# Attention probabilities as the stationary operand of the values' matmuls, softmax shares and output norms applied by token, the compressed step moved to fifth place, and the first scores issued among the latent keys' scalings

## The reference

```python
# A: 8 heads of width 64, three branches, causal:  p = softmax(q k^T * scale);  o = p v
out_a = g0 * o_cmp + g1 * o_slc + g2 * o_win    # 31 compressed keys; 512 keys; 512 keys
# B: 8 latent (mla) heads, keys and queries of width 96, values of width 64, causal
mixed = concat([rmsnorm(o_a) * out_gain_a, rmsnorm(o_b) * out_gain_b]) @ w_out
h = x + mixed                                   # then h + peer_ffn(rmsnorm(h))
```

## Time and profile before

| | |
|---|---|
| median of 3 runs | 2412.17 us (2411.32 to 2415.41) |
| the profiled execution's own time | 2410.7 us |
| its span, from first to last instruction | 2408.7 us |
| busy: PE, DVE, ACT, POOL | 98%, 71%, 35%, 46% of the span |
| attention, first scores to the B half's first products | 968.27 to 1143.83 us |

### The profile page before, as it was taken

How to read it: one execution, slowest core, us unless ns; L and a number is a source line. 1 busy time by engine, 2 the same in 40 slices (tenths; PEclk the granted TensorE clock), 3 DMA queues, 4 the chain that set the end, 5 groups by cost and what they waited for, 6 DMA issues and landing times.

```text
span 2408.7 us, 35086 instructions
## 1 busy us (share of the span) xinstructions
PE 2372.0 (98%) x12248; PEld 2033.5 (84%) x12248; DVE 1720.4 (71%) x2873; ACT 837.2 (35%) x1445; POOL 1115.0 (46%) x747
## 2 busy tenths in 40 slices
PE   8999999999999999899999999999999999999999
PEld 6888888878888887676889999999999888888887
DVE  8888785463433656876627699798886788888887
ACT  4132222100113315776224333344443333333333
POOL 7777776665666550103563788731112322222220
PEclk9999999999999999899999999999999999999999
DMA  4333323333332223100224899999999999999995
GB/s 158 97 105 105 104 95 126 134 111 108 132 117 95 88 74 121 36 1 10 70 88 127 286 311 303 301 354 347 339 342 402 383 356 349 353 358 354 346 359 200
DMA packets 181333, 490.41 MB, mean 204 GB/s; under 512 B 14848, under 2 KB 80512, under 8 KB 181248
## 3 DMA queue, kind: packets, MB, share of 16 engines
q1 hardware_dynamic: 144384, 355.12, 43.3%
q0 software_dynamic: 36864, 134.23, 14.9%
HBM read 436.86 MB, written 52.43 MB: 203 GB/s over the span
## 4 chain that ended last, share of the span: by engine, by line
PE 90%; issue 3%; POOL 3%; DVE 2%; ACT 1%; DMA 0%; SPq 0%; DVEq 0%; POOLq 0%; ACTq 0%
PE ps L690 40%; PE ps L1299 22%; PE ps L1259 17%; POOL spl L2661 2%; PE ps L1135 2%; PE ps L1280 2%; PE ps L1109 1%; POOL rare L2671 1%; PE ps L1094 1%; PE ps L874 1%; PE ps L1048 1%; PE ps L994 1%; PE ps L894 0%; PE ps L1098 0%; PE ps L1097 0%
## 5 line engine op out<-in xcount | busy, mean ns | idle before, releaser
L690 PE MATMUL ps<-hh,spl 128*128 128x512 f32 x1728 | 536.3, 390 | 4.3 <-DVE hl L2315 2.8
L1259 PE MATMUL ps<-hh,spl 128*128 128x384 f32 x2048 | 535.6, 337 | 2.9 <-POOL spl L2661 2.9
L1299 PE MATMUL ps<-spl,wsp 128*128 128x512 f32 x2304 | 523.8, 389 | 0.0
L1651 ACT ACTIVATE spl<-ring 128x1024 fp32r<-128x1024 f32 x256 | 271.9, 1062 | 678.0 <-PE ps L1299 325.6
L1299 PEld LDWEIGHTS ps<-spl,wsp 128*128 128x128 f32 x2304 | 432.0, 188 | 89.4
L2534 POOL TENSOR_TENSOR spl<-ring,spl 128x1024 fp32r<-128x1024 f32 (+1 forms) x164 | 425.6, 2595 | 13.1
L690 PEld LDWEIGHTS ps<-hh,spl 128*128 128x128 f32 x1728 | 324.3, 188 | 74.0 <-DVE hl L2315 4.2
L1259 PEld LDWEIGHTS ps<-hh,spl 128*128 128x128 f32 x2048 | 371.2, 188 | 6.3 <-issue 5.4
L2532 POOL CAST spl<-ring 128x1024 fp32r<-128x1024 f32 (+1 forms) x164 | 190.0, 1159 | 353.2 <-PE ps L690 334.6
L1259 PE MATMUL ps<-hl,spl 128*128 128x384 f32 x1024 | 342.5, 334 | 0.0
L2433 DVE TENSOR_TENSOR spl<-ring,spl 128x1024 fp32r<-128x1024 f32 x192 | 235.2, 1225 | 148.2 <-ACT spl L1651 134.3
(11 more groups left out here) (451 smaller groups left out, 3401.5 us busy)
## 6 DMA issues: line engine op xcount, KB each, us to landing
ring<-stream_in SPq DMA_DIRECT2D x134, 512.0 KB
ring<-u_in SPq DMA_DIRECT2D x128, 512.0 KB
ring<-v_in SPq DMA_DIRECT2D x128, 512.0 KB
ring<-stream_in SPq DMA_DIRECT2D x60, 704.0 KB
gelu<-gst SPq DMA_DIRECT2D x128, 192.0 KB
dense<-stage SPq DMA_DIRECT2D x12, 2048.0 KB
gl<-gelu SPq DMA_DIRECT2D x32, 768.0 KB, 7.1
gw<-dense SPq DMA_DIRECT2D x32, 768.0 KB, 9.9
```

Source lines behind the costliest of these rows:

```text
L690: m = pe.matmul(ps[:, bank, :], w[:, part, k0 + k * n:k0 + k * n + P], rhs(k), start=first and k == 0 and part == 0 and rhs is high, stop= ...
L1259: m = pe.matmul(ps[:, bank, 0:TD], w[:, part, k0 + k * P:k0 + (k + 1) * P], rhs(k), start=first and k == 0 and part == 0 and rhs is high, ...
L1299: m = pe.matmul(ps[:, bank, :], wsp[:, j % 2, part, tok], spl[:, j % 2, row, cols], start=False, stop=last and n == 2)
L1651: eng.activation(spl[:, j % 2, 0, 0:D], ring[:, j % RING, 0:D], ACT.Copy).then_inc(hi_done, 1)
```

## The change

1. **Values turned.** `values(u)` takes 128x128 tiles of turned probabilities as the stationary operand and 64 columns of V as the moving one. A slc, win or mla step on tile qt has qt+1 such matmuls, issued in pass u+3 for that step alone; cmp has one with 256 columns in place of four with 128. The result has tokens on the partitions.
2. **Shares by token.** `inverses` and `shares` are gone. `turn` waits for the exp and no longer for the shares. `weigh_head` on DVE, once for each head and branch and eight steps after its last one, takes the inverse of four sums, times the gate, and multiplies 128x256 out of PSUM; for slc and win it also adds to `oall`.
3. **Turned probabilities leave PSUM on two engines.** Tiles 0 and 1 and cmp are copied by DVE (five steps later on its list), tiles 2 and 3 by ACT (two steps later, before: four).
4. **Norms by token.** Squares with row sums run on ACT (`o_squares_of`), the inverse root makes four diagonal matrices on DVE (`turned_by`), and PE turns and scales `oall` by matmuls with them (`turned_chunk`, four of 128 columns for each of eight chunks). ACT and DVE make high and low parts straight from PSUM. POOL's squares and parts, `o_column`, `o_rows` and `o_scaled` are gone.
5. **Order.** cmp is each A head's fifth step (before: third). The scores of steps 0 to 2 stand among the last four scalings of latent keys, with their maxima on DVE (`early_bias`); only the first cmp scores wait for `mid_ready`. After the last step the first half of unit 3 stands behind the B half's `turned_chunk`.

```diff
-        HEAD_STEPS = [(SLC, 0), (SLC, 1), (CMP, 0), (SLC, 2), (SLC, 3), (WIN, 0), (WIN, 1), (WIN, 2), (WIN, 3)]
...
+        HEAD_STEPS = [(SLC, 0), (SLC, 1), (SLC, 2), (SLC, 3), (CMP, 0), (WIN, 0), (WIN, 1), (WIN, 2), (WIN, 3)]
...
+        BANK_OF = {n: 6 + (GROUPS[n][1] == "win" if n < 3 * A_H else n % 2) for n in range(GN)}
...
+        def on_dve(u):
+            return GROUPS[STEPS[u][0]][1] == "cmp" or STEPS[u][1] < 2
...
+        TURN_LAG, VALUE_LAG, WEIGH_LAG, EARLY = 2, 3, 8, 3
+        A_SQUARES, A_ROOT = A_H * PER + 6, A_H * PER + 10
+        A_TURNS = [A_H * PER + 13 + 4 * k for k in range(TT)]
...
-            def turn(n, qt):
-                u = STEP_OF[n, qt]
-                pe.wait_ge(at_scale, u + 1)
+            def turn(u):
+                n, qt = STEPS[u]
                 if u >= 2:
...
-                        v = vm[:, kt, at // 2 * P:(at // 2 + 1) * P]
-                    else:
-                        c = (kind == "win") * P
-                        v = vtok[:, kt, c:c + P]
-                    m = pe.matmul(bank[:, kt * P:], v, pt[:, wide_of(n), kt, kt * P:],
-                                  start=kind != "win" and kt == 0, stop=kind != "slc" and kt == TT - 1)
...
+                    m = pe.matmul(out_, turned[:, 0:P], vcz[:, :, g * A_D:(g + 1) * A_D], start=True, stop=True)
...
+                    for kt in range(qt + 1):
+                        if kind == "mla":
+                            v = vm[:, kt, at * B_V:(at + 1) * B_V]
+                        else:
+                            c = (kind == "win") * P + g * A_D
+                            v = vtok[:, kt, c:c + A_D]
+                        m = pe.matmul(out_[:, qt, :], turned[:, kt * P:(kt + 1) * P], v, start=kt == 0, stop=kt == qt)
...
+            def turned_chunk(c, bank):
...
+                    m = pe.matmul(ps[:, bank, t * P:(t + 1) * P], oall[:, c // TT * TT + t, c % TT * P:(c % TT + 1) * P],
+                                  turned_by[:, t, :], start=True, stop=True)
+                m.then_inc(o_turned, 1)
...
+            scores(*STEPS[0])
+            cast(3, R_MK + 4 * TT, B_QK)
+            scores(*STEPS[1])
+            cast(3, R_MK + 5 * TT, B_QK)
+            scores(*STEPS[2])
+            for h in range(6, B_H):
+                cast(3, R_MK + h * TT, B_QK)
...
+            pe.wait_ge(root_done, 4)
+            scores(*STEPS[3])
...
+            for u in range(NS):
+                pe.wait_ge(at_exp, u + 1)
                 if u + TT < NS:
                     scores(*STEPS[u + TT])
-                elif u in FIRST_HALVES:
-                    first_half(FIRST_HALVES.index(u))
-                for n, kt in VALUES_AT.get(u, ()):
-                    output(n, kt)
-                if u < NS:
-                    turn(*STEPS[u])
+                if u >= VALUE_LAG:
+                    values(u - VALUE_LAG)
+                turn(u)
+                if u in A_TURNS:
+                    c = A_TURNS.index(u)
+                    if c == 0:
+                        pe.wait_ge(inverse_done, 5)
+                    pe.wait_ge(*slot_user(turn_slot(u, True) - 2))
+                    turned_chunk(c, turn_bank(u, True))
+            values(NS - 3)
+            values(NS - 2)
+            first_half(0)
+            values(NS - 1)
+            first_half(1)
             first_half(2)
...
+            pe.wait_ge(inverse_done, 6)
+            for c, bank in zip(range(TT, DC), (0, 5, 6, 7)):
+                turned_chunk(c, bank)
             first_half(3)
...
+            for u in range(NS + TURN_LAG):
                 if u < NS:
                     probs(*STEPS[u])
-                if TT <= u < NS + TT:
-                    turned(*STEPS[u - TT])
-                for head, n in enumerate(HEAD_LAST):
-                    if u != LAST_AT[n] + 3:
-                        continue
-                    rows = slice(head % 2 * A_D, (head % 2 + 1) * A_D)
-                    eng.wait_ge(at_pv, VALUED.index(n) + 1)
-                    eng.activation(oall[rows, head // 2, :], ps[rows, 6 + head % 2, :], ACT.Copy).then_inc(at_out, 1)
-            eng.wait_ge(at_out, A_H + B_H)
-            eng.wait_ge(sum_done, 22)
-            o_inverse_root()
-            for c in range(4, DC):
-                eng.wait_ge(o_ready, c + 1)
-                eng.activation(hh[:, c, :], oall[:, c, :], ACT.Copy).then_inc(mix_high, 1)
+                if u >= TURN_LAG and not on_dve(u - TURN_LAG):
+                    turned(u - TURN_LAG)
+                if A_SQUARES <= u < A_SQUARES + TT:
+                    eng.wait_ge(at_weighed, A_DONE)
+                    o_squares_of(u - A_SQUARES, 0, T)
+                elif u == A_ROOT:
+                    eng.wait_ge(o_squares, TT)
+                    o_inverse_root(NORM_SUMS[0])
+                elif u - 1 in A_TURNS:
...
+            eng.wait_ge(at_weighed, B_DONE)
+            for t in range(TT):
+                o_squares_of(2 * TT + t, early, T, t * P)
+            eng.wait_ge(o_sum, 1)
+            o_inverse_root(NORM_SUMS[1])
+            for c, bank in zip(range(TT, DC), (0, 5, 6, 7)):
+                part_high(c, bank, hh[:, c, :])
...
+            early_bias(0)
             inverse(slice(R_KC, R_KC + 1), 4, A_G * N_CMP)
-            for h in range(4, B_H):
-                head_scaled(h)
+            head_scaled(4)
+            early_bias(1)
+            head_scaled(5)
+            head_scaled(6)
+            early_bias(2)
...
+            def weigh_head(n):
+                g, kind, at = GROUPS[n]
+                total, part = totals[:, 0, n % 8, :], totals[:, 1, n % 8, :]
+                out_, tmp = head_rows(n), weighted[:, WEIGHED[n] % 2, :, :]
+                every_column = part.unsqueeze(2).to_broadcast([P, TT, A_D])
+                dve.wait_ge(at_exp, END_OF[n] + 1)
+                if kind == "cmp":
+                    step(dve.tensor_scalar(total, total, 1e-20, None, ALU.max))
+                step(dve.reciprocal(part, total))
+                if kind != "mla":
+                    col = 2 * P + (g * A_R + at) * 3 + ("cmp", "slc", "win").index(kind)
+                    step(dve.tensor_tensor(part, part, vtok[:, :, col:col + 1].rearrange("p t c -> p (t c)"), ALU.mult))
+                dve.wait_ge(at_pv, END_OF[n] + 1)
+                if kind in ("cmp", "mla"):
+                    dve.tensor_tensor(out_, region(n), every_column, ALU.mult).then_inc(at_weighed, 1)
+                else:
+                    step(dve.tensor_tensor(tmp, region(n), every_column, ALU.mult))
+                    dve.wait_ge(at_weighed, WEIGHED[n] - 1)
+                    dve.tensor_tensor(out_, out_, tmp, ALU.add).then_inc(at_weighed, 1)
...
-                        o = dve.tensor_scalar(p_, p_, s_[:, 2:3], vtok[:, qt, col:col + 1], ALU.mult, ALU.mult)
-                o.then_inc(at_scale, 1)
...
+                dve.tensor_copy(pt[:, u % TT, 0:nk], ps[:, turn_bank(u), 0:nk]).then_inc(at_ev_dve, 1)
...
+                step(dve.reciprocal(rn[:, 0, :], rn[:, 0, :]))
+                for t in range(TT):
+                    m = dve.tensor_scalar(turned_by[:, t, :], cc("ident"), rn[:, 0, t:t + 1], None, ALU.mult)
...
+                dve.scalar_tensor_tensor(out=row, in0=ps[:, bank, :], scalar=pc("out_gain", at=c), in1=high.bitcast(F32),
+                                         op0=ALU.mult, op1=ALU.subtract).then_inc(mix_low, 1)
...
+            for u in range(NS + WEIGH_LAG - 1):
+                if EARLY <= u < NS:
                     top = step.mark(tops(*STEPS[u]))
-                if u >= LAG:
-                    inverse_at = step.mark(inverses(*STEPS[u - LAG]))
-                if u < NS:
+                if 0 <= u - TT - 1 < NS and on_dve(u - TT - 1):
+                    evacuate_turned(u - TT - 1)
+                if EARLY <= u < NS:
                     step.meet(top)
                     biases(*STEPS[u])
-                if u >= LAG:
-                    step.meet(inverse_at)
-                    shares(*STEPS[u - LAG])
-                if u == COLUMN_A + TT + 1:
+                for n in END_AT.get(u - WEIGH_LAG, ()):
+                    weigh_head(n)
+                if u == A_INVERSE:
                     o_inverted(1)
-                elif u in SCALED_A:
-                    o_scaled(SCALED_A.index(u), rstd[:, :]).then_inc(o_ready, 1)
+                elif u - TT - 1 in A_TURNS:
+                    c = A_TURNS.index(u - TT - 1)
+                    part_low(c, turn_bank(u - TT - 1, True), a_parts[c][1], a_parts[c][0])
...
-                        tile_squares(0, 0, True)
-                        for tile in range(1, 3):
-                            step(tile_squares(tile, 0, False))
-                        tile_squares(3, 0, False).then_inc(o_sum, 1)
-                        pool.wait_ge(o_sum, 1)
+                    pool.wait_ge(at_weighed, 3 if c == 2 else A_DONE)
...
-                    tile_squares(4, 1, True)
-                    step(tile_squares(5, 1, False))
```

(31 more changed lines are left out.)

293 lines of the change are left out of this document (120 added, 173 removed).

## The result

The changed kernel takes 2400.16 us, the median of 5 runs (2397.76 to 2403.66), for 2412.17: a ratio of 0.9949 with a 95% interval of 0.9935 to 0.9964, faster by more than the 0.2% that the prediction set as the bound. The forecast was 2400.9. The profiled execution took 2400.16 itself, with a span of 2398.3 us, 10.4 less than before.

A forecast was written before the change was run, and what follows sets the result against it. PE, busy for 98% of the span, was taken as the bound. Gains 8.1 + 2.5 - 2.4 + 3.1 = 11.3 us off 2410.7 give 2399.4; with the median 1.5 above, 2400.9, range 2390 to 2413.

The forecast's parts named there:

- A heads, PE's work: In A heads, slc and win branches stay at 2.4 us, cmp falls from 0.89 to 0.49; work 11.4 a head.
- A heads, the waits: In A heads, waits fall from 0.8 to 0.15 us a head, making a head 11.55; stage gain 8.1 us.
- The start: From the first scores to pass 7: PE reaches pass 7 at 980.8 for 983.3, gain 2.5 us, bounds 0 and 4.3.
- The mla steps: From 1069.74 to 1118.96 us: 3.7 us gone, 6.1 new, of it 1.8 stall; loss 2.4, bounds 0.5 and 5.
- that danger: The clock falling among the A heads, each 10 us at 1.2 GHz costing up to 5; a sign of being wrong.
- The reason that I gave for the stall: In the mla steps, ACT needs 9.2 us for squares, exps, copies, root and table loads; PE's five passes take 7.4.
- Behind the last step: From the last scores to the B half's first product: 22.4 us for 25.5, gain 3.1, bounds 2 and 4.
- The stated condition: Behind the last step, first halves cover inverse and chunk parts; without cover, each us of the chain's excess costs PE 1 us.
- The sum: Over the whole kernel, the four terms give 11.3 us off the profiled execution's 2410.7.
- new waits: Rival, chance 0.22: DVE copies behind weigh_head hold turns, the root stalls 2 us more, the start gives 0; 2409.9 us.
- The dear values' matmul: Rival, chance 0.13: a values' matmul costs over 0.222 us; 0.27 turns the gain to none, 0.31 gives 2422 us.
- More came: Rival, chance 0.15: the start's clock stays up and a values' matmul is at its lower bound; 18 us gained, 2394.

The follow-up runs named there:

- Half the columns: Changed kernel, but each slc, win and mla values' matmul moves 32 of its 64 columns of V; 2403.75 us, ratio 0.9959.
- the copy alone: Kernel before the change, with ACT copying the turned probabilities of step u-3, not u-4, behind the exp of step u; 2404.8 us, ratio 0.9969.
- copies all on ACT: Changed kernel, but ACT copies every tile of turned probabilities and DVE none; 2397.34 us, ratio 0.9941.
- root apart: Changed kernel with the root of the A norm, its inverse and its turned chunks three steps later; 2402.64 us, ratio 0.9957.

## Why the prediction was right, step by step

- **A heads, PE's work**: 2.4 a branch forecast, 0.225 a matmul or 2.25 measured; an A head has two such branches. The 0.04 of hand-over that I added four times a branch doesn't come: the matmul's 0.222 of the earlier trace rows holds amid other work as it stands. Half the columns confirm that width isn't the term. So the change's narrower matmuls are no gain by their width, as forecast.
- **A heads, the waits**: 0.15 a head forecast, none measured. A head is 11.20, not 11.55, and the stage gained 10.4, not 8.1. The mechanism was right, the copy's lateness (0.76 by the copy alone, for the 0.8 read). That this one line would also serve the other stages, 7.8 us in all, was not seen. DVE's load was sized too low, though: it is busy for 24.28 of 30 us, 0.81, where I counted 8.0 of 11.4, 0.70. It didn't matter.
- **The start**: 2.5 forecast, 2.9 measured; undoing the early scores costs 1.7 to 2.9 (23.45 less 21.72 to 20.56), the clock's part in it included. The clock's mean over the first 15 us was 0.89, so it was down for less than I took. The waits for the shares, 2.2 us of this stage before, were missing from my list. That POOL's pair would still hold DVE was seen; it cost a wait of 1.94.
- **The mla steps**: a loss of 2.4 forecast, 4.0 measured. The stall is 1.62 for 1.8. Without it, by the root one pass later, the loss is 50.48 - 49.22 - 0.47 = 0.8, for the 0.6 of the sum. The term that I left out is the clock that falls behind the stall, 1.55. I had put that danger among the A heads only. The reason that I gave for the stall, ACT's load from pass 78 on, is at most a part of it (one square, 0.6): moved away from the squares, the stall grew to 2.23, and one pass later, behind the same squares, it was 0.47.
- **Behind the last step**: 3.1 forecast, 3.18 and the two waits of 0.58 measured, 3.8. The chunks take 3.5 for 3.7, the stretch ahead of them 15.3 (1113.37 to 1128.69) for 15.8. The stated condition, that the first half of unit 3 is needed as cover, was wrong: without it nothing waits. What the gain is made of are waits: before, this stretch held 1.09 for the shares, 0.41 for a copy and 2.23 for the low parts, 3.7 in all, and now none.
- **The sum**: 11.3 forecast, 12.0 in the medians. In the profiled executions attention gave 14.1. The forecast's time is nearer than its terms, and that it came within 0.8 us is luck: three gains were 0.4 to 2.3 us too small, one loss 1.6 too small, and the untouched code ahead of attention was 3.7 us later in the second profile. The spans of the two profiles differ by 10.4 for that reason; the medians' 12.0 and the last batch's 13.8 lie between this and 14.1, and with one profile of before the rest stays open.
- **Rivals**: new waits did not eat the gain in the A heads; the one that came, at the root, was in the sum. The dear values' matmul (0.27 or more) is excluded by 0.225. More came in the A heads, but the start's clock did not stay wholly up.

The rows that show where the last stretch ends:

```profile
1113.37 1.02 PE L1124 MATMUL ps<-mqk 96*128 96x512 f32 x2
...
1128.69 3.74 PE L1167 MATMUL ps<-turned_by,oall 128*128 128x128 f32 x32
1132.19 1.86 PE L726 MATMUL ps<-oah,w 128*128 128x512 f32 x7
...
1135.06 0.40 PE L726 MATMUL ps<-hh,spl 128*128 128x512 f32 x1
```

## What to carry to other kernels

Ask of a short wait that comes back in every round whether the copy behind it can stand one step sooner on its own list; here that one line held 4.6 of 10.4 us, before any new layout. On an engine that feeds the bound one in strict order, put a table switch where the next result is due latest, and cut a neighbour's long instruction into pieces that the slack covers: these two moves together took a further 6.1 to 7.7 us off, for the change's 12.0. Compare executions by stages between fixed marks, since code that nobody touched moved by up to 5.8 us, and put the clock beside each stage. And try the one-line mend by itself first: here it brought 7.8 us over the four stages, where the whole change brought 12.5.

## What was unexpected of the hardware

The granted clock fell to 0.50 behind a stall of 1.62 us (1084 to 1088) in one kernel and stayed there to 1094 in another with a stall of the same length. It did not fall behind one of 1.79 us at the same place (`copies all on ACT`), nor behind one of 2.23 us (`root apart`, where its stage took 51.14). So the length of a single gap doesn't tell whether the clock falls, and beside itself it cost between nothing and 4.7 us.

Nor does it take a gap: in six of 13 profiles the clock fell between 830 and 845 us with PE listed as busy for 15.00 of 15.00. Just before, PE had made 24 records of one moving column (833.10 to 835.94 in the changed kernel); the same 24 ran in the seven profiles where the clock stayed up. Each of these readings is of one execution, and what decides between the two outcomes stays open.
